# Pre-norm weights applied to the columns of the turned x, x updated in place, shorter GpSimd steps in the norms, and attention probabilities turned in transpose mode

## The reference, cut to what matters

```python
def rmsnorm(x, gain):
    y = xf * lax.rsqrt(jnp.mean(xf * xf, axis=-1, keepdims=True) + NORM_EPS)
    return y * gain

for i in range(DEPTH):                       # DEPTH = 2
    x = x + 0.5 * rmsnorm(swiglu(rmsnorm(x, norms[0]), ffn_w_in[0], ffn_w_out[0]), norms[1])
    x = x + rmsnorm(mixer(rmsnorm(x, norms[2])), norms[3])
    x = x + 0.5 * rmsnorm(swiglu(rmsnorm(x, norms[4]), ffn_w_in[1], ffn_w_out[1]), norms[5])
```

## Time and profile before

| | |
|---|---|
| median of 3 runs | 1140.12 us (1139.19 to 1141.64) |
| the profiled execution's own time | 1138.89 us |
| its span | 1137.1 us |
| TensorE busy | 95% of the span |
| VectorE, ScalarE, GpSimd busy | 58%, 44%, 21% |

### The profile page before, as it was taken

One profiled execution on the slowest core, in us unless ns is written; L12 is line 12 of the kernel. 1 busy time (PEld: TensorE's weight loads), 2 busy tenths in 40 slices (PEclk: granted clock), 3 DMA queues, 4 the chain that ended last, 5 costly groups with the idle time before them and its releaser, 6 DMA issues.

```text
span 1137.1 us, 14812 instructions
## 1 busy us (share of the span) xinstructions
PE 1080.0 (95%) x5403; PEld 897.1 (79%) x5403; DVE 661.2 (58%) x693; ACT 503.8 (44%) x612; POOL 233.5 (21%) x285
## 2 busy tenths in 40 slices
PE   7999999879989999989999998999999988999997
PEld 5888887768778888868888886778889866888885
DVE  5644545846585455476554558685764558455454
ACT  5443444443354444444444445775522235444442
POOL 7700000631351000025000004153344243000000
PEclk9999999999999999999999999999999999999999
DMA  9756555421265555636556542643400024655640
GB/s 320 239 189 186 183 186 183 165 95 37 82 211 189 190 182 186 198 130 229 188 186 208 175 161 90 244 156 140 148 1 1 1 75 146 211 181 186 206 159 37
DMA packets 124696, 178.63 MB, mean 157 GB/s; under 512 B 7312, under 2 KB 98672, under 8 KB 124656
## 3 DMA queue, kind: packets, MB, share of 16 engines
q1 hardware_dynamic: 121824, 171.00, 45.4%
q0 software_dynamic: 1584, 5.77, 1.4%
q10 hardware_dynamic: 1248, 1.31, 0.4%
HBM read 177.01 MB, written 1.05 MB: 157 GB/s over the span
## 4 chain that ended last, share of the span: by engine, by line
PE 80%; DVE 10%; POOL 4%; ACT 3%; issue 2%; DMA 1%; DVEq 0%; POOLq 0%; SPq 0%; ACTq 0%
PE banks L925 15%; PE banks L927 15%; PE banks L926 15%; PE banks L956 7%; PE banks L961 7%; PE banks L958 7%; PE banks L1210 6%; DVE w_low L1415 2%; DVE x_gained L1460 2%; PE banks L990 2%; DVE mixer_arena L1427 1%; PE banks L1179 1%; ACT squares L646 1%; ACT w_high L617 1%; POOL pow_base L435 1%
## 5 line engine op out<-in xcount | busy, mean ns | idle before, releaser
L1415 DVE TENSOR_TENSOR w_low<-w_raw,w_high 128x2048 fp32r<-128x2048 f32 x160 | 376.5, 2357 | 222.6 <-ACT w_high L623 182.4
L925 PE MATMUL banks<-w_high,xT_high 128*128 128x512 f32 (+1 forms) x880 | 350.9, 399 | 7.9 <-DVE xT_low L1422 5.3
L927 PE MATMUL banks<-w_high,xT_low 128*128 128x512 f32 (+1 forms) x880 | 344.1, 391 | 0.0
L926 PE MATMUL banks<-w_low,xT_high 128*128 128x512 f32 (+1 forms) x880 | 343.3, 390 | 0.0
L623 ACT ACTIVATE w_high<-w_raw 128x2048 fp32r<-128x2048 f32 x108 | 206.4, 1911 | 113.4 <-PE banks L961 111.2
L925 PEld LDWEIGHTS banks<-w_high,xT_high 128*128 128x128 f32 x880 | 167.1, 190 | 44.4 <-DVE xT_low L1422 7.3
L927 PEld LDWEIGHTS banks<-w_high,xT_low 128*128 128x128 f32 x880 | 166.5, 189 | 35.3
L926 PEld LDWEIGHTS banks<-w_low,xT_high 128*128 128x128 f32 x880 | 167.1, 190 | 32.2
L435 POOL TENSOR_SCALAR pow_base<-y_sumsq 128x1 f32<-128x1 f32 x12 | 5.6, 470 | 658.7 <-ACT squares L646 658.7
L956 PE MATMUL banks<-w_high,hT_high 128*128 128x512 f32 x320 | 124.8, 390 | 0.0
L958 PE MATMUL banks<-w_low,hT_high 128*128 128x512 f32 x320 | 124.5, 389 | 0.0
(11 more groups left out here) (216 smaller groups left out, 1024.2 us busy)
## 6 DMA issues: line engine op xcount, KB each, us to landing
w_raw<-in_l_ffn_w_in SPq DMA_DIRECT2D x172, 512.0 KB, 4.7
w_raw<-in_l_ffn_w_out SPq DMA_DIRECT2D x88, 512.0 KB, 3.9
w_raw<-in_b_w_in SPq DMA_DIRECT2D x32, 512.0 KB, 4.5
gain_rows<-in_l_norms POOLq DMA_DIRECT2D x11, 512.0 KB, 7.3
w_raw<-in_a_w_in SPq DMA_DIRECT2D x10, 512.0 KB, 4.1
w_raw<-in_a_w_out SPq DMA_DIRECT2D x8, 512.0 KB, 6.3
w_raw<-in_b_w_out SPq DMA_DIRECT2D x8, 512.0 KB, 3.8
w_raw<-in_l_ffn_w_in SPq DMA_DIRECT2D x8, 256.0 KB, 6.1
```

The costliest lines, as they stand in the source:

```text
L925: pe.matmul(dst, sh, wh, start=start, stop=False)
L926: pe.matmul(dst, sh, wl, start=False, stop=False)
L927: return pe.matmul(dst, sl, wh, start=False, stop=stop)
L1415: dve.tensor_tensor(wlo[:, c % 3, :], raw[:, c % 3, :], whi[:, c % 3, :], ALU.subtract).then_inc(w_lo, 1)
```

## The change

Four things change.

1. All pre-norm and post-norm weights are also fetched with channels in rows (`gain_raw`, 96 rows of 128, two transfers of 24 KB), turned once by TensorE and copied to `gcol` (128 partitions x 96 columns). `turn_x` turns `xs` itself, and the pre-norm weight, now one value to a partition, is multiplied in `turned`: ScalarE makes four activations of 128x128 with a scale in place of one of 128x512, and VectorE four scalar_tensor_tensor of 128x128 (PSUM times weight minus high part) in place of one tensor_tensor of 128x512.
2. `update` replaces `next_input`, ScalarE's and GpSimd's part of the residual, and `base_of_next`: VectorE makes y x yrs x post-norm weight and adds it to `xs` in place, for both tiles, and TensorE turns the halves of `xs` as they are ready (`x_half`). GpSimd loads one broadcast weight row for a stage, not two.
3. The scale 1/D of the mean squares and the factor COEF move into the squares' own `scale` (ScalarE) or `scale=1.0 / D` (VectorE), so that `yrs` takes two GpSimd steps in place of three; GpSimd no longer waits for itself behind `rstd_ready` and `yrs_ready`. VectorE's sum of squares of tile 1 stands before the last `turned`, ScalarE's of tile 0 before its third.
4. In the attention the three matmuls against `ident` become `pe.transpose`.

```diff
@@ gpsimd
-            def base_of_next(n, kind):
-                if kind == "gdn":
-                    pool.wait_ge(c3["r1"], NG)
-                pool.wait_ge(gain_in[0], 16 * (n + 1))
-                pool.wait_ge(gain_in[1], 16 * (n + 1))
-                pool.tensor_tensor(gpair[kind], gain[:, 0, :], gain[:, 1, :], ALU.mult).then_inc(base_ready, 1)
-                pool.wait_ge(xT_ps, 4 * TBASE[n + 1])
-                for t in range(TT):
-                    pool.tensor_tensor(xg[:, t, :], xs[:, t, :], gain[:, 0, :], ALU.mult).then_inc(base_ready, 1)
...
-                power(rstd[:], xss[:], 1.0 / D, EPS, TT).then_inc(rstd_ready, 1)
-                pool.wait_ge(rstd_ready, n + 1)
...
+                link(pool.tensor_scalar(pwv[:, 8:8 + TT], xss[:], EPS, None, ALU.add))
+                pool.tensor_tensor(rstd[:], pwv[:, 8:8 + TT], mhalf[:, 0:TT], ALU.pow).then_inc(rstd_ready, 1)
+                if n and n + 1 < len(stages):
+                    pool.wait_ge(x_half, updated(n, 1))
+                    gain_load(n + 1)
...
                 for t in range(TT):
                     pool.wait_ge(ysq, TT * n + t + 1)
-                    power(yrs[:, t:t + 1], yss[:, t:t + 1], 1.0 / D, EPS, 1, COEF[n]).then_inc(yrs_ready, 1)
-                    pool.wait_ge(yrs_ready, TT * n + t + 1)
-                if n + 1 < len(stages):
-                    pool.wait_ge(ys_done, n + 1)
-                    link(pool.tensor_tensor(junk[:, 0, :], junk[:, 0, :], gain[:, 1, :], ALU.mult))
-                    pool.tensor_tensor(xs[:, 0, :], xs[:, 0, :], junk[:, 0, :], ALU.add).then_inc(x_new[0], 1)
+                    link(pool.tensor_scalar(pwv[:, 12 + t:13 + t], yss[:, t:t + 1], EPS / COEF[n] ** 2, None, ALU.add))
+                    pool.tensor_tensor(yrs[:, t:t + 1], pwv[:, 12 + t:13 + t], mhalf[:, 0:1], ALU.pow
+                                       ).then_inc(yrs_ready, 1)
@@ scalar
-            act.dma_start(gain[:, 0, :], l0_norms[0].partition_broadcast(P)).then_inc(gain_first, 16)
+            for i, w in enumerate((l0_norms, l1_norms)):
+                act.dma_start(gain_raw[6 * KT * i:6 * KT * (i + 1), :], w.rearrange("g (k p) -> (g k) p", p=P)
+                              ).then_inc(gain_cols_in, 16)
@@ turned
+                if ti in TBASE:
...
+                    for k in range(4):
+                        col = 2 * KT * n + 4 * h + k
+                        last = act.activation(xh[:, 4 * h + k, t * P:(t + 1) * P], PS[:, 6 + h, k * P:(k + 1) * P],
+                                              ACT.Copy, scale=gcol[:, col:col + 1])
+                    last.then_inc(xT_hi, 1)
+                    return
@@ tensor, attention
-                            last = pe.matmul(PS[:, 2 + g % 2, i * P:(i + 1) * P], pr[:, g % 3, i * P:(i + 1) * P],
-                                             ident[:], start=True, stop=True)
+                            last = pe.transpose(PS[:, 2 + g % 2, i * P:(i + 1) * P],
+                                                pr[:, g % 3, i * P:(i + 1) * P], ident[:])
@@ tensor, start
+            pe.wait_ge(gain_cols_in, 32)
+            pe.transpose(PS[:, 5, 0:12 * KT], gain_raw[0:12 * KT, :], ident[0:12 * KT, 0:12 * KT]
+                         ).then_inc(gain_cols_ps, 1)
@@ vector
+                if ti in TBASE:
...
+                    for k in range(4):
...
+                        last = dve.scalar_tensor_tensor(out=xl[at], in0=PS[:, 6 + h, k * P:(k + 1) * P],
+                                                        scalar=gcol[:, col:col + 1], in1=xh[at],
+                                                        op0=ALU.mult, op1=ALU.subtract)
...
+            def update(n, t, done):
+                made = scaled(n, t)
+                for h in range(2):
+                    cols = slice(h * 512, h * 512 + 512)
+                    dve.wait_ge(dve_own, made[h])
+                    dve.tensor_tensor(xs[:, t, cols], xs[:, t, cols], tmp[:, h, :], ALU.add).then_inc(done, 1)
...
                 if n:
-                    next_input(n - 1, 0)
+                    update(n - 1, 0, x_half)
                     turned(ti, 0)
                     lo(UBASE[n] + 1, 1)
                     turned(ti, 1)
-                    next_input(n - 1, 1)
+                    update(n - 1, 1, x_half)
+                    dve.wait_ge(x_half, updated(n, 1))
```

More of the change, by code:

```diff
@@ L185, in build @@
         baT = cacc[0:2 * GH, 0, :]
-        gpair = {kind: view(11264, D) for kind in ("ffn", "swa")}
-        gpair["gdn"] = vb[:, 1, :]
         Nm = xg[:, :, :].rearrange("p t d -> p (t d)").rearrange("p (b n) -> p b n", b=4)
@@ L206, in build @@
         y_ready, ysq, yrs_ready = sem("y_ready"), sem("y_squared"), sem("y_scale_ready")
-        base_ready, ys_done = sem("x_base_ready"), sem("y_scaled")
-        x_new = [sem(f"x_new{t}") for t in range(TT)]
+        x_half = sem("x_new_half")
         h_ready, silu_done, g_done = sem("h_ready"), sem("silu_done"), sem("gated_done")
@@ L669, in square_x @@
                 if n:
-                    act.wait_ge(x_new[0], n)
+                    act.wait_ge(x_half, updated(n, 0))
                 else:
                     act.wait_ge(x_in[0], 16)
-                act.activation(junk[:, 0, :], xs[:, 0, :], ACT.Square, accum_out=xss[:, 0:1]).then_inc(xsq[0], 1)
+                act.activation(junk[:, 0, :], xs[:, 0, :], ACT.Square, scale=1.0 / 32, accum_out=xss[:, 0:1]
+                               ).then_inc(xsq[0], 1)
             def enter(n):
@@ L683, in enter @@
                     turned(ti, 1)
-                    act.wait_ge(yrs_ready, TT * (n - 1) + 1)
-                    act.activation(junk[:, 0, :].rearrange("p (a b) -> p a b", a=2), PS[:, 0:2, :], ACT.Copy,
-                                   scale=yrs[:, 0:1]).then_inc(ys_done, 1)
+                    square_x(n)
                 else:
@@ L931, in turn_x @@
                 t, h = order(ti, m)
-                pe.wait_ge(xg_ready, 4 * ti + m + 1)
+                src = xs
+                if ti in OUT_INPUTS:
+                    src = xg
+                    pe.wait_ge(xg_ready, 4 * OUT_INPUTS.index(ti) + m + 1)
+                elif ti == 0:
+                    pe.wait_ge(x_in[t], 16)
+                else:
+                    pe.wait_ge(x_half, 4 * (TBASE.index(ti) - 1) + m + 1)
                 if t:
@@ L1449, in second_piece @@
                                   ).then_inc(w_lo if i else second_lo, 1)
-            def next_input(n, t):
-                dve.wait_ge(base_ready, 3 * (n + 1))
-                if t:
-                    dve.wait_ge(xg_ready, 4 * TBASE[n + 1] + 2)
-                made = [scaled(n, t, gpair[stages[n]], tmp[:, h, :], h) for h in range(2)]
-                for h in range(2):
-                    cols = slice(h * 512, h * 512 + 512)
-                    dve.wait_ge(dve_own, made[h])
-                    dve.tensor_tensor(xg[:, t, cols], tmp[:, h, :], xg[:, t, cols], ALU.add).then_inc(xg_ready, 1)
             def enter(n):
@@ L1488, in enter @@
-                made = []
-                for h in range(2):
-                    if n:
-                        made.append(scaled(n - 1, 1, gain[:, 1, :], junk[:, 1, h * 512:h * 512 + 512], h))
-                        if h == 0:
-                            turned(ti, 2)
-                if n == 0:
-                    turned(ti, 2)
-                for h in range(2):
-                    if n:
-                        cols = slice(h * 512, h * 512 + 512)
-                        dve.wait_ge(dve_own, made[h])
-                        ins = dve.tensor_tensor(xs[:, 1, cols], xs[:, 1, cols], junk[:, 1, cols], ALU.add)
@@ L1503, in enter @@
+                turned(ti, 2)
+                dve.tensor_tensor_reduce(out=junk[:, 1, :], in0=xs[:, 1, :], in1=xs[:, 1, :], scale=1.0 / D,
+                                         scalar=0.0, op0=ALU.mult, op1=ALU.add,
+                                         accum_out=xss[:, 1:2]).then_inc(xsq[1], 1)
                 turned(ti, 3)
-                if n:
-                    dve.wait_ge(x_new[1], n)
-                dve.tensor_tensor_reduce(out=junk[:, 1, :], in0=xs[:, 1, :], in1=xs[:, 1, :], scale=1.0, scalar=0.0,
-                                         op0=ALU.mult, op1=ALU.add, accum_out=xss[:, 1:2]).then_inc(xsq[1], 1)
@@ L1780, in _ @@
                     dve.wait_ge(x_out, 2)
-                made = [scaled(n, t, gain[:, 1, :], tmp[:, h, :], h) for h in range(2)]
-                for h in range(2):
-                    cols = slice(h * 512, h * 512 + 512)
-                    dve.wait_ge(dve_own, made[h])
-                    dve.tensor_tensor(xs[:, t, cols], xs[:, t, cols], tmp[:, h, :], ALU.add).then_inc(x_out, 1)
+                update(n, t, x_out)
 _INS = ["x", "positions", "l0_norms", "l0_ffn_w_in", "l0_ffn_w_out", "a_w_in", "a_b_in", "a_sinks", "a_w_out",
```

93 lines of the change are left out of this document (44 added, 49 removed).

## The result

The changed kernel takes 1114.24 us, the median of 4 runs, beside 1140.59 us of before: a ratio of 0.9767 (95% interval 0.9748 to 0.9786). I had forecast 1124, from 1117 to 1131.

The account below looks back on a forecast made before the run. TensorE, busy 95% of the span, was taken as the bound. Gains of 3.6 + 3.6 + 4.6 + 3.0 + 0.5 + 0.3 = 15.6 us off 1138.89 gave 1123.3; with the median 1.2 higher, forecast 1124 us, range 1117 to 1131.

Parts of the forecast that it names:

- Inside the ffn loops there are none: TensorE's stands: claimed only at the five stage entries, q's first turn, gdn's projections and the start.
- dropping `base_of_next` ... cost nothing: GpSimd's multiplications: counted free because GpSimd stood idle most of each ffn; no gain forecast.
- Stage 1: swa before the attention: earlier rstd starts rotations sooner, shortening the stand before q's turn; 3.6 us, from 2 to 5.3.
- The entries of stages 2, 3, 5: Stage entries: tile 1's first product comes 1.2 us earlier at each, 3.6 us together.
- the relief from GpSimd: Entries: VectorE's addition takes 1.28 us instead of 4.34; without it the entry would be 1.9 us later than before.
- Attention: Transposes for products against ident: TensorE-bound step falls from 2.33 to 2.0 us; 4.6 us in all, ceiling 5.4.
- gdn's entry and load: Stage 4: entry 1.2, earlier weight load takes 1.4 off a 2.13 us wait, low part 0.4; 3.0 us.
- The start: First weights: dearer turned adds 0.6, dropping a 512 KB broadcast helps; between +0.6 and -1.4, taken as -0.5 us.
- The pieces of `turned`: Entries and start: four pieces per engine take 1.14 + 1.11 us instead of 0.60 + 0.69, 0.96 more a turn.
- Rival (b): turned's pieces cost more at 17 places: gain gone at 0.9 us more a turn (3%); milder part shares 24%.
- Rival (d): More gain: the stand before q's turn nearly goes, clock stays, start loads win 1.4; 1119 us, 11%.
- Rival (c): Attention: transposes let the clock fall to 1.2 GHz, 32 us more, 1156 us; 4% shared with the pieces' worst case.

Follow-up runs that it names:

- a_bmixmm: Changed kernel with attention products against ident and GpSimd's two multiplications put back beside the swa and gdn out-projections: 1122.62 us (0.9853).
- a_mm: Changed kernel with the products against ident put back in the attention: 1119.25 us (0.9814).
- a_sq: Changed kernel with VectorE's sum of squares of tile 1 put back behind the fourth low part of every entry: 1119.76 us (0.9814).
- a_one: Changed kernel with the turned x taken in one piece per engine, leaving out the pre-norm weights (prices only): 1105.16 us (0.9693).
- a_add: Changed kernel with two GpSimd instructions over 1024 columns, result unread, put at every entry: 1119.44 us (0.9811), two of seven executions at 1145.
- b_pt: Kernel before with one edit, the attention's probabilities turned by transposes instead of products with ident: 1136.63 us (0.9965).
- a_gbmm: Changed kernel with the 512 KB weight broadcast back at the start and attention products against ident: 1120.90 us (0.9838).
- a_again: The changed kernel itself, unchanged, run once more: 1114.97 us (0.9780), five of five at full clock.
- a_gb: Changed kernel with the 512 KB weight broadcast put back as the start's first transfer: one execution 1117.25 us, three about 1142.4.
- a_bmix: Changed kernel with GpSimd's two multiplications put back beside the swa and gdn out-projections alone: 1144.86 us, attention at half clock.
- v_mix: Changed kernel with first and third turn of an entry, and one at the start, weighted through SBUF: five of six executions 1135.5 to 1136.5 us, one 1112.46.
- v_tr: Changed kernel with first and third turns at entries of stages 1 to 5 through SBUF, all transposes kept: 0.9742; five 1109.58 to 1112.62 us, two 1135.9.
- a_base: Changed kernel with GpSimd's two multiplications of x by a weight row put back, ffn included, result unread: 1129.98 us (0.9908).
- v_sb: Changed kernel with VectorE writing every weighted turned tile to SBUF, then ScalarE and VectorE working on halves by turns: 1128.17 us (0.9892).
- v_mm: Changed kernel with first and third turns at entries of stages 1 to 5 through SBUF and attention products against ident: 1117.26 us (0.9796).

## Why the prediction was off

The direction and most mechanisms were right; the sum was 10 us too small. By its terms:

- **The stands were listed incompletely.** The step that failed outright is the sentence "Inside the ffn loops there are none. They lie at the five entries of a stage, at the first turn of q, in gdn's projections, and at the start". The two out-projections had one each of 1.58 us, and gdn has others that the change leaves alone. With it "dropping `base_of_next` ... cost nothing" missed a gain of 3.4 us (`a_bmixmm` against `a_mm`), 3.6 by the leads. This term was put at nothing though the waits before named it.
- **Stage 1: 3.6 forecast, 6.2 to 6.6 found.** I took 3.0 for the rotations from a range of 2 to 4, and half of the clock's 1.2. The stand fell by 4.16 us, the lead by 4.7 up to q's turn, and all of the clock's price came back (1.5). `a_sq` shows the order of the sum of squares as the cause, `a_one` that it takes the fall of the low parts as well; that it fell so well is luck.
- **The entries of stages 2, 3, 5: 1.2 each forecast, 1.6 to 1.9 found** (5.3 in all, not 3.6). The rebuilt walk from turn to product was right to 0.1 us (11.32 found; 509.1 - 497.67 = 11.43 forecast), though its stands were not all so (0.23 and 0.21 us where I had 0.55 and 0.65); the shorter steps of `yrs` and what follows the fourth low part gave the rest. `a_add` shows that I had the relief from GpSimd too dear.
- **Attention: 4.6 forecast**, 5.0 (`a_mm`), 4.0 (`b_pt`), 5.1 by the leads.
- **gdn's entry and load: 3.0 forecast, 3.7 found** (the rest of the row's 5.0 is stage 3's). TensorE waits 0.5 us at 704.19 where it waited 2.13. The number is about right, the reason isn't: I had the load come earlier because `rstd` does, and in `a_sq`, with `rstd` only 15.3 us ahead of that product (17.0 before the change, 18.9 with it), the wait is 0.50 us too. What shortened it (one broadcast beside the load where there were two, for one) no run tells apart.
- **The start: 0.5 forecast, 0.9 to 1.2 found**; `a_gbmm` gives the broadcast 1.7 us. A start is not steady, though: in `a_again` TensorE waits 1.97 us for x at 19.57, where the first profile shows 0.64.
- **The pieces of `turned`**: 2.25 us forecast for a pair, 2.26 found. Rival (b) is out.

Rival (d) had the right size for stage 1; the range ended 3 us above the result because no case held the out-projections. Rival (c), which I gave less than 4%, is real, and came in one of nine executions of the changed kernel, by its time and mean clock. I had argued that ordinary products are most of a step's work; that does not protect it. Its mechanism is shown in part only (last section). Its price, which I put at 32 us, is 25.

## What to carry to other kernels

Before costing the removal of work on GpSimd at nothing, list every VectorE instruction that runs beside it and look for one that is longer there than elsewhere (3.41 against 2.29 us here), then ask who waits for that one; and go through the list of TensorE's waits to its end, asking of each what made the operand late. Both stands were in it, as waits for `w_low`, and I had passed them over. An instruction on VectorE that feeds a chain over GpSimd can be worth moving ahead even of TensorE's next operand: one swap was 5 us, where the low parts then missed most of the chain. And a change that turns matmuls into transposes is to be timed over many executions: its median can look like a plain gain while some executions give all of it back.

## What the runs showed of the hardware

A stretch dense in transposes may run at 1.2 GHz from end to end. In the five profiles that caught it (`a_add`, `a_gb`, `a_bmix`, `v_mix`, `v_tr`) the granted clock is 0.50 through the attention, a step takes 3.58 us and not 1.94, and the clock is back during the out-projection, whose products are nearly all ordinary. But the fall comes ahead of that stretch. In all five it shows in the same eight turns of q, when only the first three turns of probabilities have run; `a_bmix` and the changed kernel there, with the same stands (0.84 us ahead, and 0.58 or 0.57):

```profile
238.58 1.97 PE L1109 MATMUL banks<-ident,mixer_arena 128*128 128x128 f32 x8 [0.58 <-POOL mixer_arena L459]
```

```profile
237.99 1.09 PE L1102 MATMUL banks<-ident,mixer_arena 128*128 128x128 f32 x8 [0.57 <-POOL mixer_arena L458]
```

With products in place of the transposes the stand ahead of these eight is shorter (0.17 to 0.19 us). So the pairs below differ in two things, and no run tells whether it is the transposes themselves or this stand that lets the clock fall; with the transposes it did not come back in some 50 us of a busy TensorE.

Executions 23 to 26 us above the others, at a mean granted clock 0.02 to 0.03 lower, were 20 of 44 of the kernels with three transposes a step and a short stand before the first turn of q, 0.94 to 1.76 us (the changed kernel 1 of 9, `a_base` 2 of 6, `a_add` 2 of 7, `a_gb` 3 of 4, `a_bmix` 5 of 5, at 1142 to 1147 us with none to compare, `v_mix` 5 of 6, `v_tr` 2 of 7), 2 of 12 with one product of three, and none of 19 with products in their place. That the attention is where these others lost their time was seen in the profiled ones alone. `b_pt`, `a_sq`, `a_one` and `v_sb` have the transposes and none in 18; all four have a longer stand before the first turn of q (5.1, 5.1, 4.1 and 4.3 us, where the changed kernel has 0.97), with a short fall of the clock in their profiles that was over by 241 us. Why that goes with a kept clock stays open. The Trainium skill says ("TensorE: Matmul & The Clock Gate", Part 4: PE-mode transpose) that transposes don't count as TensorE activity in the same way; the pairs `a_gb` and `a_gbmm`, `v_tr` and `v_mm` agree with it as far as they go, and the executions at full clock show that it doesn't decide alone.

VectorE and GpSimd held each other up as if they worked by turns: in `a_base` a low part that takes 2.29 us elsewhere took 7.40 beside GpSimd's two multiplications (4.71), though it had started 0.53 us before them.
